# Next hgrn head's projections and gate chain between the present head's levels, with a second buffer set

## The chip, the core and the metric

The kernel runs on one core of one Trainium2 chip, as one launch. The metric is the device time of that execution in microseconds. The core has five engines that run in parallel, each in its own order: TensorE (PE, matmuls; its weight loads are PEld), VectorE (DVE), ScalarE (ACT), GpSimd (POOL) and SyncE (SP, here the issuer of weight loads). They meet at semaphores: an instruction that waits holds up all that is queued behind it on its engine. PSUM is the memory that matmuls write; everything else works in SBUF.

## The reference, cut to what matters

Two blocks run one after the other on a sequence of 512 tokens of width 1024. The first has two layers of mixed attention. The second, where the change lies, has three branches from one normalised input `h`, gated and summed, and then an FFN:

```python
o_a = dsa_attention(...)                    # sparse attention over selected keys
o_b = hgrn2_mixer(bq, bf, bi, bg, ...)      # 4 heads, gated linear recurrence in chunks of 64
o_c = mla_attention(...)                    # latent attention, 4 heads
gates = jax.nn.sigmoid(gate_logits)         # 3 x 1024 columns of h @ w_in
mixed = g_a * (o_a @ w_up_a) + g_b * (o_b @ w_up_b) + g_c * (o_c @ w_up_c)
x = x + mixed @ w_out                       # then the FFN and a last norm
```

Of the hgrn branch, for each head (keys and values of 128):

```python
log_f = jnp.logaddexp(log_lb, jnp.log1p(-lb) + jax.nn.log_sigmoid(fr))
k_in = (1.0 - lb) * jax.nn.sigmoid(-fr)
b = jnp.cumsum(lfc, axis=2)                                  # within a chunk
o_inter = jnp.einsum('bhck,bhkv->bhcv', qc * jnp.exp(b), state)
attn = jnp.einsum('bhtk,bhsk,bhtsk->bhts', qc, kc, decay)    # decay = exp(b_t - b_s), s <= t
new_state = exp(b_last) * state + einsum(kc * exp(b_last - b), vc)
o = rms_norm(o, out_gain) * jax.nn.silu(g)
```

## The kernel before

All activations stand transposed, with the feature on the 128 partitions and the 512 tokens along the row. `plan` writes out one list of steps by hand, and each engine's program is a walk through that list (`for op, arg in steps`) that takes from each step the part that is its own. So the order of steps is the order of every engine's queue.

**Groups.** A PE product that fills one PSUM bank is a `group`. There are two banks, `proj0` and `proj1`, used in turn: group g waits until whoever reads group g-2 has read it. A projection of 8 slabs of input (K=8) is 24 matmuls of 128x512 (L1436), since operands are split into a rounded part and a rest: high by high, high by low, low by high. Its weights come by one DMA of SP (L1316, 512 KB), are rounded by ACT (L1900) and subtracted by POOL (L1378) into the rest; `place_splits` puts that rounding (`split`) into the list some two groups ahead, but never ahead of the step in a slab's `after`.

**One hgrn head** has these steps, all of them 128x512:
- Projections of its queries (`hgrn_q`, "hq") and forget logits (`hgrn_f`, "hf"), evacuated by ACT (L1683).
- The gate chain: `hg_gate_a` part 0 on ACT (L1640 to L1642: abs, exp, ln), `hg_gate_d` part 0 on DVE (L2281 to L2283), `hg_gate_a` part 1 on ACT (L1866, then L1640 to L1642), `hg_gate_d` part 1 on DVE (L2288 to L2291, with a scan over tokens).
- Levels -1 to 5. The decay within a chunk is split by powers of two: for a level, DVE takes differences (`hg_diff`, L2300, L2301), ACT exponentials (L1872, L1873), DVE multiplies queries and keys by them (`hg_level`, L2314, L2315), PE multiplies these 4 times 128x128 (`hg_attn`, L1503), and DVE copies the product under a mask into the head's scores (`hg_put`, L2325). `hgrn_level` asks for the factors of the level after the one whose product it issues.
- The end: `hg_decay` (ACT L1880, L1881; DVE L2332, L2333), `hg_turn` (PE L1509, ACT L1731), two `hg_state` groups (PE L1519), `hg_chain` (DVE L2342, L2344), the head's gate projection `hgrn_gate` with silu (ACT L1640 to L1642, DVE L1997, ACT L1748, DVE L2047), `hg_out` (PE L1528, L1532; ACT L1733, L1737), `hg_meansq` (PE L1472), `hg_norm` (ACT L1646, L1647; DVE L2354), `gate3` (DVE L2057).

In `hgrn_state` and `hgrn_out` the next head's two projections and its gate chain stand between these.

**Tail gates.** The 24 K=8 projections of the branch gates ("sigmoid" groups) are spread evenly over the jobs. Gate i is copied by ACT into one of two buffers (L1729), goes through abs, exp, ln (ACT), min and subtract (DVE L2039) and exp (ACT L1745) in the steps `sig_ln`, `sig_min`, `sig_out` of the next gates, and is stored by a DMA of POOL (L1374). Its buffer serves gate i+2, whose copy waits for that DMA.

**Attention.** 16 tiles of latent attention (kind M) and 16 of sparse attention (kind X) run as a pipeline: `tick` issues one step of it, scores of tile n (PE L1572 to L1574 or L1576), softmax on DVE and ACT (L2095 to L2127, L1770; L2108, L2109, L1767), transposes of tile n-3 (PE L1588, ACT L1792), product with the values of tile n-4 (PE L1602). `weave` hands out ticks between jobs by a credit that each job's weight earns. All 32 tiles are through during the second head, at 1324 us.

**After it.** The step `tail` on ACT waits for all of this. Then ACT and DVE split ya, and the `up` groups follow.

## Time and profile before

| | us |
|---|---|
| median of the runs (2034.4 to 2037.26) | 2035.2 |
| profiled execution, its own time | 2032.24 |
| its span | 2030.4 |
| PE busy, of the span | 1764.3 (87%) |
| DVE busy | 847.8 (42%) |
| ACT busy | 805.0 (40%) |
| POOL busy | 590.5 (29%) |

Busy time counts an engine's instructions of work; waiting for a semaphore is not in it. The clock column (PEclk) is the mean of TensorE's granted clock in a stretch, 1 being full. An idle time in brackets stands behind the row that it ended with, with the engine and line that released it. Of a wait for several semaphores the last one is named. In the chain of work that ended last, 69% of the span is PE, 13% DVE, 8% ACT. Tile names are those of memory, so the same name can be different things: `weights` is the arena in which hgrn's buffers lie, `constants` also the tail gates, `h_tok` also the latent attention's queries and keys, `E` and `index_and_shared` two more buffers.

### The profile page before, as it was taken

The page shows a single profiled execution, that of the slowest core. Times are in us where ns is not written, and L with a number is a line of the kernel's source. Part 1 is how long each engine was busy: PE and PEld are TensorE (multiplying, and loading weights), DVE is VectorE, ACT ScalarE, POOL GpSimd, SP SyncE. Part 2 cuts the span into 40 slices and gives each one's busy share as a digit, 9 for nine tenths or more (in the row PEclk, how much of TensorE's full clock was granted, in tenths as well). Part 3 has the DMA queues.
Part 4 walks back from the last instruction along what each step waited for, and adds up shares of the span by engine and source line. Part 5 has one row for each costly group of instructions (what it writes and reads, how often), then busy time and mean ns, then how long its engine had stood idle before and what let it go on. Part 6 is the DMA issues. An engine that isn't in the chain of part 4 may idle for free.

```text
span 2030.4 us, 20883 instructions
## 1 busy us (share of the span) xinstructions
PE 1764.3 (87%) x7694; PEld 1325.3 (65%) x7694; DVE 847.8 (42%) x1477; ACT 805.0 (40%) x1512; POOL 590.5 (29%) x291
## 2 busy tenths in 40 slices
PE   4899998889989988889979968867769879999997
PEld 3666765667757656676636657656557658888886
DVE  4363345453433453544983536242326312212401
ACT  2234447322344563433324545453443324434411
POOL 4332211144122211422201222131236424444540
PEclk8898999999989988899989989888879989999999
DMA  5312221023132201231212222221245323333221
GB/s 172 88 42 63 63 59 57 22 64 93 32 82 54 83 32 43 88 82 33 60 36 58 73 73 63 60 66 48 66 132 185 103 62 100 98 94 101 86 94 42
DMA packets 204115, 149.83 MB, mean 74 GB/s; under 512 B 14956, under 2 KB 183536, under 8 KB 204016
## 3 DMA queue, kind: packets, MB, share of 16 engines
q1 hardware_dynamic: 199488, 133.57, 23.3%
q0 software_dynamic: 4528, 14.95, 2.4%
q8 instruction: 62, 1.02, 0.2%
q14 instruction: 37, 0.30, 0.0%
HBM read 138.00 MB, written 10.49 MB: 73 GB/s over the span
## 4 chain that ended last, share of the span: by engine, by line
PE 69%; DVE 13%; ACT 8%; issue 4%; DMA 3%; SPq 1%; POOL 0%; ACTq 0%; DVEq 0%
PE proj L1436 39%; PE proj L1432 12%; PE attn_out L1602 3%; PE score L1559 3%; PE score L1622 2%; PE turned_probs L1588 2%; PE proj L1622 1%; ACT weights_rounded L1900 1%; PE attn_out L1622 1%; DMA weights_raw<-in_w_in 1%; DVE small L2157 1%; DMA gates<-constants 1%; SPq L1316 1%; DVE rel_bias L2070 1%; PE score L1563 1%
## 5 line engine op out<-in xcount | busy, mean ns | idle before, releaser
L1378 POOL TENSOR_TENSOR weights_rounded<-weights_raw,weights_rounded 128x1024 fp32r<-128x1024 f32 (+1 forms) x237 | 562.8, 2392 | 1140.3 <-ACT weights_rounded L1900 1140.2
L1436 PE MATMUL proj<-hT_high,weights_rounded 128*128 128x512 f32 x2336 | 785.7, 410 | 47.4 <-DVE weights L2325 16.6
L1436 PEld LDWEIGHTS proj<-hT_high,weights_rounded 128*128 128x128 f32 x2336 | 456.9, 196 | 163.3 <-issue 20.4
L1436 PE MATMUL proj<-hT_low,weights_rounded 128*128 128x512 f32 x1168 | 468.9, 401 | 0.0
L1900 ACT ACTIVATE weights_rounded<-weights_raw 128x1024 fp32r<-128x1024 f32 (+1 forms) x237 | 233.9, 1009 | 161.1 <-DMA weights_raw<-in_w_ffn_down 57.8
L1436 PEld LDWEIGHTS proj<-hT_low,weights_rounded 128*128 128x128 f32 x1168 | 229.2, 196 | 50.4 <-issue 4.7
L1432 PE MATMUL proj<-weights_rounded,hT_high 128*128 128x512 f32 (+1 forms) x640 | 212.3, 409 | 43.8 <-DVE hT_low L1981 21.0
L1432 PEld LDWEIGHTS proj<-weights_rounded,hT_high 128*128 128x128 f32 x640 | 127.9, 203 | 77.3 <-issue 23.4
L1588 PE MATMUL turned_probs<-constants,probs 128*128 128x128 f32 x320 | 62.1, 296 | 43.4 <-ACT probs_T L1792 43.0
L1640 ACT ACTIVATE tg<-proj 128x512 f32<-128x512 f32 x42 | 25.1, 598 | 177.0 <-PE proj L1436 177.0
L1559 PE MATMUL score<-qk 64*128 64x256 f32 (+3 forms) x256 | 81.0, 495 | 11.0 <-DVE qk L1975 8.2
L1602 PE MATMUL attn_out<-probs_T,V 128*64 128x128 f32 (+1 forms) x560 | 89.5, 295 | 0.0
L1602 PEld LDWEIGHTS attn_out<-probs_T,V 128*64 128x64 f32 (+1 forms) x560 | 70.1, 173 | 10.9 <-issue 9.2
L1432 PE MATMUL proj<-weights_rounded,hT_low 128*128 128x512 f32 (+1 forms) x192 | 75.5, 393 | 0.0
L2019 DVE SCALAR_TENSOR_TENSOR tg<-proj,tg 128x512 f32<-128x512 f32 x22 | 15.2, 692 | 142.2 <-ACT tg L1642 142.2
L1436 PE MATMUL proj<-branches_high,weights_rounded 128*128 128x512 f32 x192 | 61.8, 398 | 13.0 <-POOL weights_rounded L1378 10.8
L1588 PEld LDWEIGHTS turned_probs<-constants,probs 128*128 128x128 f32 x320 | 37.6, 150 | 51.7 <-DVE probs L2127 30.6
L1374 POOL DMA_DIRECT2D gates<-constants x24 | 13.3, 556 | 198.8 <-ACT constants L1745 198.6
L2089 DVE TENSOR_REDUCE small<-score 128x1 f32<-128x128 f32 (+3 forms) x64 | 28.3, 484 | 92.8 <-PE score L1563 92.8
L1997 DVE SCALAR_TENSOR_TENSOR tg<-proj,tg 128x512 f32<-128x512 f32 x20 | 13.8, 692 | 125.2 <-ACT tg L1642 125.2
L1683 ACT ACTIVATE qk<-proj 128x512 f32<-128x512 f32 x32 | 19.1, 597 | 109.7 <-PE proj L1436 109.7
L1559 PEld LDWEIGHTS score<-qk 64*128 64x128 f32 x256 | 30.0, 192 | 45.7 <-issue 32.0
(371 smaller groups left out, 2463.6 us busy)
## 6 DMA issues: line engine op xcount, KB each, us to landing
weights_raw<-in_w_in SPq DMA_DIRECT2D x113, 512.0 KB, 4.1
weights_raw<-in_w_out SPq DMA_DIRECT2D x24, 512.0 KB, 3.8
weights_raw<-in_w_ffn_gate SPq DMA_DIRECT2D x22, 512.0 KB, 3.8
weights_raw<-in_w_ffn_up SPq DMA_DIRECT2D x22, 512.0 KB, 3.8
weights_raw<-in_w_ffn_down SPq DMA_DIRECT2D x22, 512.0 KB, 3.6
gates<-constants POOLq DMA_DIRECT2D x24, 256.0 KB, 2.4
weights_raw<-gates SPq DMA_DIRECT2D x24, 256.0 KB, 3.9
weights_raw<-in_w_in SPq DMA_DIRECT2D x20, 256.0 KB, 3.1
```

The costliest lines, as they stand in the source:

```text
L1316: sp.dma_start(dst, src).then_inc(p["loaded"], 16)
L1378: nc.gpsimd.tensor_tensor(piece_view(WR, p, "raw"), piece_view(WF, p, "raw"), piece_view(WR, p, "high"), ALU.subtract).then_inc(w_low, 1)
L1432: mm = nc.tensor.matmul(ps[:, 0:gr["N"]], x_[:, k, t * P:(t + 1) * P], w_[:, 0:gr["N"]], start=first, stop=last)
L1436: mm = nc.tensor.matmul(ps[:, :], w_[:, c0:c0 + P], x_[:, k, :], start=first, stop=last)
L1559: nc.tensor.matmul(ps[:, 0:K], qk[r, it["q"], tq], qk[r, it["k"], 0:K], start=True, stop=False)
L1563: mm = nc.tensor.matmul(sc[b % SCORE_BANKS][:, K - P:K], identb[:, :], negb[:, int(kind == "C"), :], start=False, stop=True)
L1588: mm = nc.tensor.transpose(T[:, j * P:(j + 1) * P], PR[:, i % 3, j * P:(j + 1) * P], cn("ident"))
L1602: mm = nc.tensor.matmul(O[u % 2][r0:r0 + rn, t * P:(t + 1) * P], v, PT[:, i % 2, j * P:(j + 1) * P], start=(j == 0), stop=(j == t))
L1622: mm = nc.tensor.matmul(down[2 * t + half][:, :], x_[c][:, t * P:(t + 1) * P], w_[:, 512 * half:512 * half + 512], start=(c == 0 and j == ...
L1640: link(nc.scalar.activation(dst, src, ACT.Abs, **kw))
L1900: nc.scalar.activation(piece_view(WR, p, "high"), piece_view(WF, p, "raw"), ACT.Copy).then_inc(w_high, 1)
L2089: ins = nc.vector.tensor_reduce(nmax[:, c + j:c + j + 1], sc[(first_map[n] + j) % SCORE_BANKS][:, 0:K], AX, ALU.max, negate=True)
```

## The change

Where the code puts the next head's two projections and its gate chain is new: between the levels of the present head, instead of in its end. For this a second set of the buffers b, k and q of a head is taken (`by_head`, in `E` and in `X2`, read in the traces as `index_and_shared`), and the chain no longer uses hG and hKE. The credit of `weave` gives way to `paced`, in which each job has a number of ticks written beside it, and the tail gates stand at written places: two between the levels of a head, and up to four in its end (after level 5, after the states, after the output, after the squares). All attention tiles are now spread over the four heads. The masked copy of a level comes ahead of the next level's factors. The last two tail gates are projected after the step `tail`, behind the split of ya, and the last steps of both stand between the first `up` groups. One more buffer is cleared once, and level 0 of a head waits for the output of the head before.

```diff
+    def paced(jobs, new_items):
+
+        add_items(new_items)
+        for fn, ticks in jobs:
+            fn()
+            for _ in range(ticks):
+                if state["n"] < len(items) + DRAIN:
+                    tick()
...
     def hgrn_level(h, lv):
 
+        put_back()
         if lv + 1 < LEVELS:
             steps.append(("hg_level", (h, lv + 1)))
             steps.append(("hg_diff", (h, lv + 2)))
         else:
             steps.append(("hg_decay", h))
-        g = group("hg_attn", head=h, level=lv)
+        hold["put"] = group("hg_attn", head=h, level=lv)
+
+    def hgrn_turn(h):
         put_back()
-        hold["put"] = g
+        group("hg_turn", head=h)
+        if h < 3:
+            steps.append(("hg_diff", (h + 1, 0)))
 
     def hgrn_state(h):
-        group("hg_turn", head=h)
-        put_back()
-        if h < 3:
-            hgrn_q(h + 1)
-        gs = [group("hg_state", head=h, part=i) for i in range(2)]
-        if h < 3:
-            hgrn_f(h + 1)
-        steps.append(("hg_chain", (h, gs)))
-        hold["states"] = gs
-        if h < 3:
-            steps.append(("hg_gate_a", (h + 1, 0)))
-        hold["g"] = hgrn_gate(h)
-        if h < 3:
-            steps.append(("hg_gate_d", (h + 1, 0)))
+        hold["states"] = [group("hg_state", head=h, part=i) for i in range(2)]
+        steps.append(("hg_chain", (h, hold["states"])))
 
     def hgrn_out(h):
-        hold["hgout"] = group("hg_out", head=h, states=hold["states"])
-        if h < 3:
-            steps.append(("hg_gate_a", (h + 1, 1)))
+        group("hg_out", head=h, states=hold["states"])
+
+    def hgrn_meansq(h):
         group("hg_meansq", head=h)
+
+    def hgrn_norm(h):
         steps.append(("hg_norm", h))
         steps.append(("gate3", hold["g"]))
-        if h < 3:
-            steps.append(("hg_gate_d", (h + 1, 1)))
-            steps.append(("hg_diff", (h + 1, 0)))
...
+        put_back()
+        hold["g"] = group("gate", slab("hgrn", c0=HG + 128 * h), K=KD, chunk=4 + h, layer=l, first=False, unit=None)
+
+    def gate_step(h, *what):
+        if h < 4:
+            steps.extend((name, (h, part)) for name, part in what)
+
+    def next_f(h):
+        if h < 4:
+            put_back()
+            hgrn_f(h)
+
+    def next_q(h):
+        if h < 4:
+            put_back()
+            hgrn_q(h)
+            gate_step(h, ("hg_gate_a", 0))
+
+    given = [0]
 
     def tail_gate(i):
-        gate_ready(i - 2)
-        gate_logs(i - 1)
-        gate_out(i - 2)
+        for what, n in (("sig_min", i - 2), ("sig_ln", i - 1), ("sig_out", i - 2)):
+            if 0 <= n < N_GATES:
+                steps.append((what, n))
         if i < N_GATES:
             put_back()
             group("sigmoid", slab("gate2", at=1024 * TAIL_ORDER[i // 8] + 128 * (i % 8)), K=KD, nth=i)
...
+    def next_gate():
+        tail_gate(given[0])
+        given[0] += 1
...
-    weave(jobs, its)
-    for i in (N_GATES, N_GATES + 1):
-        tail_gate(i)
+    jobs = []
+    for h in range(4):
+        last = h == 3
+
+        def level(lv, ticks, h=h):
+            jobs.append((lambda: hgrn_level(h, lv), ticks))
+            if h == 1 and 0 <= lv < NT:
+                jobs.append((lambda: steps.append(("masked", lv)), 0))
+
+        level(-1, 1)
+        jobs.append((lambda h=h: next_f(h + 1), 0))
+        level(0, 1)
+        jobs.append((lambda h=h: next_q(h + 1), 0))
+        level(1, 0)
+        jobs.append((next_gate, 0))
+        jobs.append((lambda h=h: gate_step(h + 1, ("hg_gate_d", 0)), 0))
+        level(2, 1)
+        jobs.append((lambda h=h: gate_step(h + 1, ("hg_gate_a", 1)), 0))
+        level(3, 0)
+        jobs.append((next_gate, 1))
+        jobs.append((lambda h=h: gate_step(h + 1, ("hg_gate_d", 1)), 0))
+        level(4, 0)
+        jobs.append((lambda h=h: hgrn_gate(h), 1))
+        level(5, 1)
+        jobs.append((lambda: steps.append(("gate2", hold["g"])), 0))
+        jobs.append((next_gate, 0))
+        jobs.append((lambda h=h: hgrn_turn(h), 1))
+        jobs.append((lambda h=h: hgrn_state(h), 1))
+        jobs.append((next_gate, int(last)))
+        jobs.append((lambda h=h: hgrn_out(h), int(last)))
+        if not last:
+            jobs.append((next_gate, 0))
+        jobs.append((lambda h=h: hgrn_meansq(h), int(last)))
+        if not last:
+            jobs.append((next_gate, 0))
+        jobs.append((lambda h=h: hgrn_norm(h), 0))
+    paced(jobs, its)
     flush()
-
-
-    new_rings(RINGS_TAIL)
     state["after"] = ("tail", 0)
     steps.append(("tail", 0))
+    steps.append(("split_x", ("ya", 0, 4)))
+    while given[0] < N_GATES:
+        next_gate()
+    new_rings(RINGS_TAIL)
...
+            if b == 0 and c in (0, 2):
+                next_gate()
...
-        hF, hA, hK, hQ = (qk[:, 4 + i, :] for i in range(4))
-        hB, hG, hQD, hKE, hATT = (X[:, i, :] for i in range(5))
+        hF, hA = qk[:, 4, :], qk[:, 5, :]
+        hB0, hG, hQD, hKE, hATT = (X[:, i, :] for i in range(5))
+        by_head = [(hB0, qk[:, 6, :], qk[:, 7, :]), (E[:, 0, 1, :], E[:, 1, 1, :], ikT)]
...
@@ -1862,9 +1891,10 @@
                         wait_group(hf_group[h])
                         log1p_exp_abs(hA, hF).then_inc(hg_act, 1)
                     else:
+                        _, hK, _ = by_head[h % 2]
                         act.wait_ge(hg_dve, 2 * h + 1)
-                        nc.scalar.activation(hG, hB, ACT.Exp)
-                        log1p_exp_abs(hKE, hA).then_inc(hg_act, 1)
+                        nc.scalar.activation(hK, hK, ACT.Exp)
+                        log1p_exp_abs(hF, hA).then_inc(hg_act, 1)
...
+                    if lv == 0 and h:
+                        dve.wait_ge(group_full, out_group[h - 1] + 1)
```

What this does to the queues shows in three places. First, DVE behind the end of head 0. Before, three steps of head 1's chain stand between the gate's product (L2047) and a softmax tile:

```order
L2342 COPY raw<-proj 128x128
L2344 SCALAR_TENSOR_TENSOR raw<-raw,small,proj 128x128 x6
L1997 SCALAR_TENSOR_TENSOR tg<-proj,tg 128x512
L2047 TENSOR_TENSOR tg<-proj,tg 128x512
L2281 SCALAR_TENSOR_TENSOR qk<-qk 128x512
L2282 TENSOR_TENSOR weights<-qk 128x512
L2283 TENSOR_SCALAR qk<-qk,small 128x512
```

The state chain, the gate and then head 1's `hg_gate_d` part 0 stand in a row. A little later, still DVE before, from the norm on:

```order
L2354 SCALAR_TENSOR_TENSOR y<-y,small,tg 128x512
L2057 TENSOR_TENSOR y<-y,tg 128x512
L2288 TENSOR_SCALAR qk<-qk,small 128x512
L2289 TENSOR_TENSOR weights<-weights,qk 128x512
L2290 SCALAR_TENSOR_TENSOR weights<-chunk_keep,weights 128x512
L2291 TENSOR_SCALAR qk<-weights,small 128x512
L2300 TENSOR_TENSOR weights<-weights 128x256
L2301 TENSOR_TENSOR weights<-weights 128x256
```

Part 1 of the chain stands between the head's output and the first difference of head 1. Now, DVE from the state chain of head 0 to the first levels of head 1:

```order
L2380 COPY raw<-proj 128x128
L2382 SCALAR_TENSOR_TENSOR raw<-raw,small,proj 128x128 x6
L2126 TENSOR_REDUCE small<-score 128x1
L2127 TENSOR_SCALAR small<-small 128x1
L2151 RECIPROCAL small<-small 128x1
L2158 TENSOR_SCALAR probs<-E,small 128x384
L2070 SCALAR_TENSOR_TENSOR constants<-constants,gate_logs 128x512 x3
L2392 SCALAR_TENSOR_TENSOR y<-y,small,tg 128x512
L2088 TENSOR_TENSOR y<-y,tg 128x512
L2351 TENSOR_TENSOR weights<-index_and_shared,weights 128x256
L2352 TENSOR_TENSOR weights<-E,weights 128x256
L2334 TENSOR_TENSOR weights<-E 128x256
```

The chain is gone from here; three tail gates (L2070) stand in its place, and the first level follows the output at once. The chain of head 1 is found further up on DVE, between levels of head 0:

```order
L2362 COPY_PREDICATED weights<-level_masks,proj 128x512
L2313 SCALAR_TENSOR_TENSOR E<-qk 128x512
L2314 TENSOR_TENSOR E<-E,qk 128x512
L2315 TENSOR_SCALAR qk<-E,small 128x512
L2351 TENSOR_TENSOR z<-qk,weights 128x32x8
L2352 TENSOR_TENSOR z<-qk,weights 128x32x8
L2334 TENSOR_TENSOR weights<-weights 128x256
L2335 TENSOR_TENSOR weights<-weights 128x256
```

`hg_gate_d` part 0 (L2313 to L2315) has moved between the masked copy of level 1 and the factors of level 3, and writes to `E`.

Second, ACT at the end of head 0. Now the outputs of head 0 stand among tail gates:

```order
L1758 ACTIVATE constants<-proj 128x512
L1762 ACTIVATE y<-proj 128x512
L1766 ACTIVATE tg<-y 128x512
L1669 ACTIVATE gate_logs<-constants 128x512
L1670 ACTIVATE gate_logs<-gate_logs 128x512
L1671 ACTIVATE gate_logs<-gate_logs 128x512
L1774 ACTIVATE constants<-constants 128x512
L1758 ACTIVATE constants<-proj 128x512
L1931 ACTIVATE weights_rounded<-weights_raw 128x1024
L1669 ACTIVATE gate_logs<-constants 128x512
L1670 ACTIVATE gate_logs<-gate_logs 128x512
L1671 ACTIVATE gate_logs<-gate_logs 128x512
```

Before, this was the same engine and place:

```order
L1767 ACTIVATE E,small<-logits,small 128x128
L1792 ACTIVATE probs_T<-turned_probs 128x256
L1733 ACTIVATE y<-proj 128x512
L1737 ACTIVATE tg<-y 128x512
L1866 ACTIVATE weights<-weights 128x512
L1640 ACTIVATE weights<-qk 128x512
L1641 ACTIVATE weights<-weights 128x512
L1642 ACTIVATE weights<-weights 128x512
L1900 ACTIVATE weights_rounded<-weights_raw 128x1024
L1646 ACTIVATE tg<-proj,small 128x512
L1647 ACTIVATE tg<-tg 128x512
L1872 ACTIVATE weights<-weights 128x256
```

The four steps of head 1's chain (L1866, L1640 to L1642) have gone, and copy, logarithms and exponential of the tail gates have come between output and norm.

Third, ACT ahead of the `up` groups. Before:

```order
L1729 ACTIVATE constants<-proj 128x512
L1640 ACTIVATE gate_logs<-constants 128x512
L1641 ACTIVATE gate_logs<-gate_logs 128x512
L1642 ACTIVATE gate_logs<-gate_logs 128x512
L1745 ACTIVATE constants<-constants 128x512 x2
L1916 ACTIVATE branches_high<-y 128x2048
L1900 ACTIVATE weights_rounded<-weights_raw 128x512 x9
```

and now:

```order
L1947 ACTIVATE branches_high<-y 128x2048
L1669 ACTIVATE gate_logs<-constants 128x512
L1670 ACTIVATE gate_logs<-gate_logs 128x512
L1671 ACTIVATE gate_logs<-gate_logs 128x512
L1774 ACTIVATE constants<-constants 128x512
L1931 ACTIVATE weights_rounded<-weights_raw 128x1024 x2
L1758 ACTIVATE constants<-proj 128x512
L1669 ACTIVATE gate_logs<-constants 128x512
L1670 ACTIVATE gate_logs<-gate_logs 128x512
L1671 ACTIVATE gate_logs<-gate_logs 128x512
L1774 ACTIVATE constants<-constants 128x512
L1758 ACTIVATE constants<-proj 128x512
```

The split of ya (L1916, now L1947) has moved ahead of the last two tail gates, and the rounding of those gates' weights stands behind it.

## Rows read from the trace of the kernel before

**Rows 1.** Windows: us, then busy (x) of PE, PEld, DVE, ACT, POOL; PEclk; DMA.

```profile
1081.30:1508.20 426.90, 327.81 (x1562) 260.33 (x1560) 174.36 (x364) 199.18 (x384) 95.94 (x63) 0.89 0.23 66
1081.30:1170.40 89.10, 81.73 (x396) 61.06 (x394) 44.48 (x103) 42.31 (x93) 20.67 (x13) 0.96 0.23 63
1170.40:1215.80 45.40, 28.25 (x143) 22.18 (x143) 18.29 (x41) 19.98 (x39) 9.27 (x7) 0.87 0.26 81
1215.80:1283.20 67.40, 60.58 (x321) 49.07 (x320) 35.40 (x84) 37.19 (x83) 14.62 (x10) 0.96 0.21 59
1283.20:1332.10 48.90, 29.86 (x151) 24.59 (x151) 13.96 (x26) 19.91 (x33) 9.98 (x5) 0.84 0.18 49
1332.10:1378.90 46.80, 39.12 (x181) 32.47 (x181) 21.38 (x38) 22.91 (x42) 14.52 (x9) 0.91 0.24 68
1378.90:1420.90 42.00, 31.15 (x136) 24.88 (x135) 11.61 (x20) 16.15 (x25) 7.67 (x4) 0.88 0.21 57
1420.90:1470.80 49.90, 35.61 (x157) 29.39 (x157) 19.77 (x39) 25.24 (x46) 14.60 (x10) 0.83 0.23 69
1470.80:1508.20 37.40, 21.52 (x87) 16.68 (x87) 9.48 (x15) 15.48 (x24) 4.60 (x5) 0.72 0.31 98
```

**Rows 2.** Waits of PE in 1081.3:1508.2: us in total, times, longest us.

```profile
PE turned_probs L1588 <- ACT probs_T L1792: 25.0, 9, 9.7
...
PE proj L1472 <- ACT tg L1737: 12.0, 4, 6.8
...
PE proj L1436 <- POOL weights_rounded L1378: 10.8, 1, 10.8
```

**Rows 3.** Costliest groups of PE there: busy us, mean ns, idle before.

```profile
L1436 PE MATMUL proj<-hT_high,weights_rounded 128*128 128x512 f32 x544 | 192.7, 428 | 30.3 <-DVE weights L2325 16.6 <-DVE raw L2344 11.0 <-ACT constants L1729 2.8
```

**Rows 4.** Chain that ended last, at head 2: start us, us, what.

```profile
1352.07 5.55 PE proj L1436 x24
```

**Rows 5.** Timeline, PE and ACT: start us, us, what, idle before.

```profile
1352.20 0.39 PE L1436 MATMUL proj<-hT_low,weights_rounded 128*128 128x512 f32 x1
...
1502.74 1.89 ACT L1916 ACTIVATE branches_high<-y 128x2048 fp32r<-128x2048 f32 x1
...
1508.18 0.76 PE L1436 MATMUL proj<-branches_high,weights_rounded 128*128 128x512 f32 x1 [10.82 <-POOL weights_rounded L1378]
```

**Rows 6.** Timeline of DVE at the end of head 0, and PE behind it.

```profile
1191.87 0.56 DVE L2095 TENSOR_REDUCE small<-score 128x1 f32<-128x384 f32 x1
...
1192.74 0.48 DVE L2127 TENSOR_SCALAR probs<-E,small 128x256 f32<-128x256 f32 x1
...
1205.56 1.70 DVE L2354 SCALAR_TENSOR_TENSOR y<-y,small,tg 128x512 f32<-128x512 f32 x1 [7.70 <-ACT tg L1647]
...
1207.98 0.54 DVE L2288 TENSOR_SCALAR qk<-qk,small 128x512 f32<-128x512 f32 x1
...
1213.83 0.45 PE L1588 MATMUL turned_probs<-constants,probs 128*128 128x128 f32 x1 [9.75 <-ACT probs_T L1792]
```

**Rows 7.** Timeline of ACT around one gate of the tail.

```profile
1153.38 0.61 ACT L1745 ACTIVATE constants<-constants 128x512 f32<-128x512 f32 x1
...
1157.24 0.60 ACT L1729 ACTIVATE constants<-proj 128x512 f32<-128x512 f32 x1 [3.25 <-DMA gates<-constants]
...
1160.82 1.04 ACT L1900 ACTIVATE weights_rounded<-weights_raw 128x1024 fp32r<-128x1024 f32 x1
```

**Rows 8.** Timeline of the decay's product on DVE twice, and of POOL.

```profile
1145.84 2.92 POOL L1378 TENSOR_TENSOR weights_rounded<-weights_raw,weights_rounded 128x1024 fp32r<-128x1024 f32 x1 [7.73 <-ACT weights_rounded L1900]
...
1146.44 2.88 DVE L2333 TENSOR_TENSOR qk<-qk,weights 128x512 f32<-128x512 f32 x1
...
1266.78 0.68 DVE L2333 TENSOR_TENSOR qk<-qk,weights 128x512 f32<-128x512 f32 x1
```

**Rows 9.** Costliest groups of DVE in 1081.3:1508.2.

```profile
L2300 DVE TENSOR_TENSOR weights<-weights 128x256 f32<-128x256 f32 x22 | 15.7, 712 | 0.8
...
L2354 DVE SCALAR_TENSOR_TENSOR y<-y,small,tg 128x512 f32<-128x512 f32 x4 | 5.9, 1475 | 42.4 <-ACT tg L1647 42.4
```

66 lines of the change are left out of this document (22 added, 44 removed).

## The prediction

> **What bounds the kernel now.** The page's first part has TensorE (PE) busy for 87% of the span and no other engine over 42%, so I look for the places where PE stands. The diff touches only the stretch from the first product of the hgrn levels (1081.3 us) to the first up projection (1508.2), so I cut that into windows: for each of the four heads its levels, and its end (turn, states, next head's projections, gate, output, norm) [rows 1]. In the whole stretch PE is busy 327.8 of 426.9 us, hence idle 99.1. No other engine comes near: ACT 199.2, DVE 174.4, POOL 95.9. So PE bounds it, through the waits between its groups. By difference the idle time is 7.4, 6.8, 7.7 and 14.3 us in the four levels (36.2 together), 17.1, 19.0 and 10.9 in the first three ends (47.0), and 15.9 in the last. The waits of PE say on what [rows 2]: 25.0 us before the transposes of the softmax, which are behind DVE and ACT at a head's end, 12.0 on the squares for the head's norm, 10.8 before the first up projection.
>
> The half clock takes more. Over the stretch it is 0.89 [rows 1], so of the two levels, 2.4 and 1.2 GHz, the lower was granted for 22%, 94 us. The 544 matmuls of the projections on hT_high last 428 ns on average [rows 3]; one at the upper level lasts 0.39 us and at the lower 0.76, and 24 in a row at the upper level take 5.55 us, 0.23 each from start to start [rows 4, 5]. The excess, 544 x 0.038 = 21 us of duration, and half as much again for the 272 on hT_low, makes 31 / 0.37 = 84 matmuls at half speed. Each steps 0.23 slower: 19 us, and with some of it on attention and levels about 25. In proportion that is 0.25 us for each idle us (an estimate: the clock fell in and behind the idle places), and leaves about 303 us of work at full clock. The change keeps this work: 34 projections of 24 matmuls (24 gates, 10 of hgrn), 28 level products, 32 attention tiles, four ends.
>
> **The change, part by part.**
>
> 1. *Projections of the next head, and its gate chain, leave the end.* Today the end holds two of PE's K=8 groups for the next head, and DVE has seven instructions for its chain, the last four (L2288 to L2291) just before the first level of the next head, from 1207.98, after a norm of 1.70 that waited 7.70 for ACT; PE stands meanwhile, idle 9.75 us before the transposes at 1213.83 [rows 6]. All of it moves under the levels at no cost of PE time, since each step there stands between two projections of 5.55 us; ACT's logarithms (three of 0.63 and an exponential) go along, in ACT's queue behind the evacuation of the projection. The second buffers (E, X2, the fourth slot of qk) are what lets it. Added: one memset before the stretch, which I cost at nothing because DVE is idle there between topk rounds; uncovered it is below 1 us, for head 0 only. No DMA is added. SP's loads keep their distance of two groups, so their landings stay hidden by the projections ahead.
>
> 2. *Level steps.* They keep their order, with the masked copy now always ahead of the next level's factors. PE's products need factors made one job earlier, so a projection covers the chain. What remains is ACT's queue: a gate evacuation (L1729) waits for the DMA of the gate two before it. From the exponential before (1153.38 + 0.61) it starts at 1157.24, 3.25 us later, POOL's issue included [rows 7]. A gate's turn on ACT is then 0.60 (copy) + 1.04 (rounding the next weights) + 3 x 0.63 + 0.61 + 3.25 = 7.4 us, against 5.55 of projection. Whenever other PE work between two gates is under 1.9 us, a bank is freed late. Walking the new order through one head with these durations gives 1.0 us before the product of level 3, 2.4 before the gate projection, and about 1 of crumbs: 4.5. Head 0, with few tiles yet, 4; head 3, with no next head to project, 0.8 + 2 + 1.6 and the rest of a chain that is bare in places, 9. Together 22 against 36.2. Bounds: nothing, to 14.3 for each head, the bare chain of head 3 today [rows 1].
>
> 3. *The end of heads 0 to 2.* (a) The gate group's bank is freed by DVE's product L2047, which now stands behind the decay and two attention tiles. From the end of that projection: three logarithm steps of 0.63 on ACT, 0.69 on DVE (a 128x512 pass of either is 0.60 to 0.69, [rows 6 to 8]), a softmax tile on DVE 1.3 (0.56 + 0.48 and two one-column steps, [rows 6]), its exponential and copy on ACT some 0.9, the decay's exponentials 0.85 and products 2 x 0.68, the next tile with its exponential 1.9, then 0.63 and 0.69: 10 us, against two tiles and a product on PE, some 5.4. Idle 4.6. (b) The chain of states (2.75 today, twice a bank wait on DVE) has a tile as cover: 0. (c) Three gates then stand between turn, output and squares. The first two have 3 to 4 us beside them; the third follows a short group, and its bank is 1.4 late. (d) Level -1 of the next head needs the bank of the squares, which ACT frees only behind the third gate's copy: 3.3. Sum 9.3 for each, 28 for three against 47.0. Bounds: 5 (only a) to 19.0 (as today).
>
> 4. *The last end.* Two gates move behind the tail step, and with them the rounding of their weights, since the planner puts a slab made after `tail` behind it. So after the last squares PE waits for ACT root 1.3, DVE norm and gate 1.5 to 2.4, ACT's copy of ya 1.89 [rows 5], logarithms 1.9, exponential 0.6, rounding 1.04, POOL 2.4: with waits between them 11.5, less 0.8 for the last transposes, 10.7 us idle. Today's 10.82 before the first up projection [rows 5] falls to some 3.3, because ya is split by then, and 1.3 more before the second. With (a) at 5.6 (sparse tiles are longer on DVE) and 1 before the squares: 22 against 15.9. This part loses 6. Bounds: 11 if the wait before the last two gates is hidden, 26 if that wait and today's 15.9 simply add.
>
> *Sum.* Idle 22 + 28 + 22 = 72, against 99.1: 27 less. At 0.25 for the clock that gives 7 more. **34 us.** The profiled execution took 2032.2 (span 2030.4), so 1998; it stands 3 under the median of the runs, 2035.2, from which 34 leaves **2001**.
>
> *A rule against it.* Where DVE reads two SBUF tensors while POOL subtracts, it is stretched: L2333 took 2.88 us beside a subtraction of 2.92, and 0.68 without [rows 8]. The Trainium skill, GPSIMD Engine Reference, section "Key points", has it that GpSimd shares its SBUF interfaces with VectorE and contends with such instructions; this trace agrees, at 2.88 against 0.68. The change puts the chain and levels nearer to the subtractions. By the rows what is stretched today lies in the idle times that I counted, and 34 stands; by the rule at its worst it is the third rival.
>
> **The rivals.**
>
> *Fuller cover.* If my late banks in levels are covered by PE work that I set too short, levels cost 8 instead of 22, and the ends 5 each: idle 8 + 15 + 22 = 45, 54 less, with the clock 67: 1968. For it: head 0's levels, with a tile in nearly every step, have only 7.4 idle at 0.96 clock [rows 1]. Against: the gate's turn of 7.4 us stands in ACT's queue wherever the tiles stand. 0.15.
>
> *Waits change places.* Attention is spread to the end, so heads 2 and 3 get DVE and ACT work in levels that now run bare. If each level stretch then costs what head 3's costs now, 14.3, idle is 57 + 28 + 22 = 107, 8 more: 2045. With half of that growth it is 89. For it: the two heads without attention have as much idle per level time as those with it [rows 1]. Against: the factors of a level are made one job ahead of its product in the new order. That half would be 2023. Counted under "no change": 0.08.
>
> *Slower, by stretched DVE.* POOL's 35 subtractions in the stretch each last 2.4 us. If each catches one two-input DVE instruction on the chain at 2.88 - 0.68 = 2.2 us, that is 77 us, against 10 now in the two kinds most stretched: 22 x (0.71 - 0.42) + 4 x (1.48 - 0.69) [rows 9]. It decides from 34 / 1.25 = 27 us exposed, twelve more such hits where PE waits. At full price, 67 x 1.25 = 84 less 34: 2085; at half, 2043. 0.09. For it: the norm L2354 was stretched to 1.70 in the end that I cited, and there the two engines meet by plan. Against: with a projection of cover in each step a hit of 2.2 is mostly hidden.
>
> *It doesn't do what it says:* should the new waits on the previous head's output (level 0) or the gate DMA serialise head after head, the ends stay at 47: idle 91, 10 us won: 2025. 0.06.
>
> **How the numbers follow.** Forecast 0.62 (1980 to 2020), fuller cover 0.15, little won 0.06, waits change places 0.08, slower 0.09. The range for 8 in 10 takes half of the fuller cover and of the little won: 1974 to 2031. A measurement here tells 0.2% (4 us) from no change. Faster by more: 0.62 + 0.15 + 0.06 and 0.02 of the waits that change places, 0.85; within 0.2%: 0.05 of those; slower: 0.09 and the last 0.01 of them, 0.10.
>
> **What would show it.** In the profile after: the stretch from first level product to first up projection 427 - 34 = 393 us long, PE idle about 72 in it, clock 0.91 to 0.93; the 9.75 before the transposes gone; 3 to 6 us before the gate that follows level 5; 2 to 4 before each head's level -1; some 11 us between the last attention output and the last two gate projections, at a lowered clock; the first up projection under 5 us after them. Wrong if DVE's two-input instructions with over 2 us are more than half again as many, if ACT's evacuations of gates wait for DMA over 4 us each, or if the level stretches show over 10 us idle each.

## The result, and the profile after

| | before | after |
|---|---|---|
| median of the runs, us | 2036.2 (2034.4 to 2037.5) | 2002.6 (1997.4 to 2008.3) |
| ratio to before, 95% interval | | 0.9836 (0.9808 to 0.9864) |
| span of the profiled execution | 2030.4 | 2000.8 |
| first level product to first up projection | 426.9 | 393.4 |

The prediction said 2001, with 393 us for that stage. It had 2035.2 as the median before, from three of the four runs in this table; the four give 2036.2, so the change brought 33.6 us by the medians and 29.6 by the two profiled spans. The windows of the kernel after, which answer to [rows 1], first the whole stage, then levels and end of each head in turn, and last the 20 us behind the first up projection (columns: us, busy time with instructions of PE, PEld, DVE, ACT and POOL, PEclk, DMA share, GB/s; the first tail gate behind level 5 counts to the end):

```profile
1078.80:1472.20 393.40, 325.60 (x1562) 257.93 (x1560) 193.96 (x362) 191.62 (x375) 94.09 (x60) 0.90 0.23 66
1078.80:1128.00 49.20, 45.36 (x214) 35.15 (x213) 27.10 (x51) 22.08 (x47) 10.51 (x5) 0.93 0.24 64
1128.00:1170.90 42.90, 36.31 (x174) 27.58 (x172) 13.68 (x29) 23.27 (x43) 11.90 (x8) 0.92 0.23 65
1170.90:1226.20 55.30, 49.70 (x242) 38.88 (x243) 44.02 (x77) 26.62 (x56) 13.18 (x7) 0.94 0.24 65
1226.20:1271.60 45.40, 36.67 (x175) 27.86 (x173) 13.73 (x30) 23.28 (x43) 14.03 (x12) 0.92 0.34 108
1271.60:1325.00 53.40, 46.05 (x224) 38.57 (x225) 36.33 (x61) 26.71 (x56) 13.52 (x7) 0.90 0.25 67
1325.00:1370.40 45.40, 36.16 (x168) 28.57 (x166) 15.22 (x29) 23.35 (x43) 11.92 (x8) 0.89 0.22 62
1370.40:1411.00 40.60, 35.25 (x177) 29.12 (x178) 26.45 (x54) 20.07 (x45) 8.31 (x5) 0.87 0.22 61
1411.00:1472.20 61.20, 40.09 (x198) 32.19 (x196) 17.43 (x32) 26.24 (x46) 10.72 (x8) 0.83 0.13 44
1472.20:1492.20 20.00, 13.64 (x50) 10.43 (x51) 5.76 (x7) 9.09 (x14) 10.56 (x9) 0.89 0.80 249
```

PE's idle time in the stage is 393.4 - 325.6 = 67.8 us, where it was 99.1; 72 was predicted. Its work is the same 1562 matmuls. So of the 33.5 us that the stage is shorter, 31.3 are idle time and 2.2 are matmuls that ran faster (a second profile of the same kernel, below, has 29.1 and 5.0). Behind the stage, 6.4 us were lost again: from the first up projection to the end it is 528.6 us, and it was 522.2. In the last window above PE is idle 6.4 us; in the 20 us behind the first up projection before, it was busy 19.53. The start of the stage lies 2.5 earlier, but that is chance: in the kernels of this study, which hardly differ up to there, it lies between 1072.7 and 1083.5. The waits of PE in the stage, to be read beside [rows 2] (us in total, times, longest):

```profile
PE proj L1465 <- DVE tg L2078: 15.8, 4, 4.1
PE proj L1465 <- POOL weights_rounded L1407: 12.7, 1, 12.7
PE proj L1465 <- ACT constants L1758: 10.4, 7, 2.7
PE turned_probs L1617 <- ACT probs_T L1821: 6.7, 6, 2.2
PE proj L1532 <- ACT tg L1676: 6.3, 3, 2.1
PE proj L1532 <- ACT constants L1758: 5.0, 2, 2.9
...
PE proj L1501 <- ACT tg L1766: 0.2, 1, 0.2
```

Line numbers are some 30 higher now: L1465 is the projection, L1532 the level product, L1617 the transposes, L1501 the squares of the norm, L1758 ACT's copy of a tail gate, L2078 DVE's product for the head's gate. The 25.0 us before transposes are 6.7 now, and the 12.0 before the squares 0.2. What is left is mostly the banks. Where it stands in time (start us, us, what, idle before):

```profile
1132.61 0.79 PE L1465 MATMUL proj<-hT_high,weights_rounded 128*128 128x512 f32 x1 [3.85 <-DVE tg L2078]
...
1170.92 1.16 PE L1532 MATMUL proj<-index_and_shared,E 128*128 128x128 f32 x8 [2.10 <-ACT tg L1676]
...
1455.96 0.77 PE L1465 MATMUL proj<-hT_high,weights_rounded 128*128 128x512 f32 x1 [12.69 <-POOL weights_rounded L1407]
1472.18 0.47 PE L1465 MATMUL proj<-branches_high,weights_rounded 128*128 128x512 f32 x1 [2.96 <-issue]
1481.32 0.77 PE L1465 MATMUL proj<-branches_high,weights_rounded 128*128 128x512 f32 x1 [3.36 <-issue]
1491.47 0.79 PE L1465 MATMUL proj<-branches_high,weights_rounded 128*128 128x512 f32 x1 [3.00 <-DVE V L2035]
```

These are the places that the prediction named: (a) before the gate behind level 5, (d) before level -1, the two late gates, the first up projection. For the last two rows, 6.4 us together, it had one wait of 1.3.

### The profile page after: what moved, and what is told of

Read it like the earlier page. It is cut to its first block, busy times and chain, and to the rows that moved or that the text cites. A ratio compares the mean times of both kernels' runs of the same rounds, so it can differ in the third digit from the quotient of the medians.

```text
span 2000.8 us, 20884 instructions
## 1 busy us (share of the span) xinstructions
PE 1761.0 (88%) x7694; PEld 1321.8 (66%) x7694; DVE 875.5 (44%) x1478; ACT 803.1 (40%) x1512; POOL 586.4 (29%) x291
## 4 chain that ended last, share of the span: by engine, by line
PE 69%; DVE 13%; ACT 8%; issue 4%; DMA 4%; POOL 1%; SPq 1%; ACTq 0%; DVEq 0%
PE proj L1465 39%; PE proj L1461 13%; PE attn_out L1631 3%; PE score L1588 3%; PE score L1651 2%; DMA gates<-constants 2%; PE proj L1651 2%; PE turned_probs L1617 1%; ACT weights_rounded L1931 1%; DMA weights_raw<-in_w_in 1%; PE attn_out L1651 1%; DVE small L2188 1%; POOL weights_rounded L1407 1%; DVE rel_bias L2101 1%; PE proj L1471 1%
## 5 line engine op out<-in xcount | busy, mean ns | idle before, releaser
L1465 PE MATMUL proj<-hT_high,weights_rounded 128*128 128x512 f32 x2336 | 785.4, 410 | 60.0 <-POOL weights_rounded L1407 20.3
L1465 PEld LDWEIGHTS proj<-hT_high,weights_rounded 128*128 128x128 f32 x2336 | 456.4, 195 | 177.3 <-issue 31.9
L1465 PE MATMUL proj<-hT_low,weights_rounded 128*128 128x512 f32 x1168 | 469.1, 402 | 0.0
L1465 PEld LDWEIGHTS proj<-hT_low,weights_rounded 128*128 128x128 f32 x1168 | 229.1, 196 | 49.3 <-issue 3.9
L1617 PE MATMUL turned_probs<-constants,probs 128*128 128x128 f32 x320 | 59.8, 287 | 26.4 <-ACT probs_T L1821 26.2
L2050 DVE SCALAR_TENSOR_TENSOR tg<-proj,tg 128x512 f32<-128x512 f32 x22 | 15.2, 692 | 141.9 <-ACT tg L1671 141.9
L1465 PE MATMUL proj<-branches_high,weights_rounded 128*128 128x512 f32 x192 | 63.1, 406 | 11.5 <-issue 6.3
L1617 PEld LDWEIGHTS turned_probs<-constants,probs 128*128 128x128 f32 x320 | 36.6, 146 | 33.7 <-DVE probs L2158 14.1
L1793 ACT ACTIVATE E<-score,small 128x128 f32<-128x128 f32 (+3 forms) x64 | 33.2, 524 | 60.0 <-DVE small L2120 60.0
L1821 ACT ACTIVATE probs_T<-turned_probs 128x128 f32<-128x128 f32 (+3 forms) x128 | 54.2, 423 | 4.1 <-PE turned_probs L1617 4.1
```

Of the source, the lines that this page charges most:

```text
L1465: mm = nc.tensor.matmul(ps[:, :], w_[:, c0:c0 + P], x_[:, k, :], start=first, stop=last)
L1617: mm = nc.tensor.transpose(T[:, j * P:(j + 1) * P], PR[:, i % 3, j * P:(j + 1) * P], cn("ident"))
L1793: ins = nc.scalar.activation(e[:, j, :], sc[(first_map[n] + j) % SCORE_BANKS][:, 0:K], ACT.Exp, bias=nmax[:, c + j:c + j + 1], accum_out=s ...
L1821: nc.scalar.activation(PT[:, i % 2, 0:it["K"]], T[:, 0:it["K"]], ACT.Copy).then_inc(turned_out, 1)
```

## The experiments

Each starts from the kernel after, but for the last. The stage is counted from the first level product to the first up projection.

| kernel | median us | ratio to before (95%) | stage us | PE idle | PE busy | PEclk |
|---|---|---|---|---|---|---|
| before (profiled as above) | 2031 to 2033 | 1 | 426.9 | 99.1 | 327.8 | 0.89 |
| after_again | 2001.6 | 0.9843 (0.9813 to 0.9872) | 392.8 | 70.0 | 322.8 | 0.91 |
| chain_back | 2045.7 | 1.0067 (1.0042 to 1.0093) | 433.2 | 98.6 | 334.6 | 0.87 |
| tiles_early | 2031.2 | 0.9992 (0.9972 to 1.0012) | 424.3 | 89.9 | 334.5 | 0.88 |
| tail_undo | 1991.2 | 0.9799 (0.9777 to 0.9820) | 384.6 | 63.4 | 321.2 | 0.91 |
| tail_split | 1995.8 | 0.9827 (0.9799 to 0.9855) | 382.8 | 64.8 | 318.0 | 0.92 |
| gate2_early | 1999.1 | 0.9842 (0.9813 to 0.9871) | 390.2 | 66.1 | 324.1 | 0.91 |
| three_buffers | 1987.7 | 0.9783 (0.9752 to 0.9815) | 374.6 | 57.6 | 317.0 | 0.91 |
| three_tail | 1968.0 | 0.9694 (0.9663 to 0.9725) | 360.4 | 46.3 | 314.1 | 0.93 |
| gate2_three_tail | 1953.0 | 0.9612 (0.9590 to 0.9634) | 340.0 | 31.6 | 308.4 | 0.96 |
| all_late | 1954.7 | 0.9619 (0.9599 to 0.9639) | 338.4 | 32.5 | 305.9 | 0.97 |
| pool_light | 1992.0 | 0.9800 (0.9772 to 0.9828) | 380.0 | 60.2 | 319.8 | 0.92 |
| before_light | 2022.4 | 0.9949 (0.9929 to 0.9968) | 424.6 | 90.1 | 334.5 | 0.87 |

The common measure, the kernel after once more:

> The changed kernel as it is, timed beside the others, as their common measure: 0.984 of the kernel before, about 2002 us. Its stage from the first level product to the first up projection about 393 us, PE idle 68 in it.

It came to 2001.6, and its stage to 392.8 us. Two profiled executions of the same kernel thus differ by 2.2 us in idle time and 2.8 in busy time. Smaller differences in the table say nothing. The largest difference is in the levels of head 3, 5.4 us idle in the kernel after and 9.7 in after_again (the window as in the table of windows above, and a PE instruction in it):

```profile
1364.80:1407.10 42.30, 32.62 (x177) 26.95 (x178) 26.59 (x54) 20.07 (x45) 8.35 (x5) 0.96 0.21 59
...
1386.11 1.16 PE L1532 MATMUL proj<-z 128*128 128x128 f32 x8 [2.70 <-ACT constants L1758]
```

It is 42.3 us long instead of 40.6, at a granted clock of 0.96 instead of 0.87, with 32.6 us busy instead of 35.3. The 2.70 are for a gate's copy whose buffer was stored in 4.5 us; the same store took 2.3 in the kernel after. Where another engine sets the pace, slower matmuls fill time in which PE would else be idle, so idle and busy time of a short stretch can't be read apart.

### The two halves of the change

chain_back puts the next head's projections and chain back into the end:

```diff
     def hgrn_state(h):
+        if h < 3:
+            hgrn_q(h + 1)
         hold["states"] = [group("hg_state", head=h, part=i) for i in range(2)]
+        if h < 3:
+            hgrn_f(h + 1)
         steps.append(("hg_chain", (h, hold["states"])))
+        gate_step(h + 1, ("hg_gate_a", 0))
...
-        jobs.append((lambda h=h: next_f(h + 1), 0))
...
-        jobs.append((lambda h=h: next_q(h + 1), 0))
...
+        jobs.append((lambda h=h: gate_step(h + 1, ("hg_gate_d", 1), ("hg_diff", 0)), 0))
```

> Undoes the main part alone: the next head's two projections and its gate chain stand in the end of the present head again, at the places they had before (queries' projection before the states, forget logits behind them, chain around gate, output and norm). Second buffers, spread tiles, tail gates at their written places and the tail stay as in the changed kernel. Theory (the gain came from projections and chain under the levels): levels are barer and the next head waits for the chain again, 20 to 35 us slower than the changed kernel, that is as slow as the kernel before or slower. Rival (spread tiles and written places of the gates brought most of it): under 8 us slower.

It took 2045.7 us, 44 more than the kernel after and 0.67% more than before, above the 20 to 35 of the theory. The chain is bare between norm and level -1 again. Timeline of DVE and of PE in chain_back at the end of head 0:

```profile
1183.32 0.75 DVE L2393 SCALAR_TENSOR_TENSOR y<-y,small,tg 128x512 f32<-128x512 f32 x1 [15.18 <-ACT tg L1677]
...
1184.78 0.54 DVE L2322 TENSOR_SCALAR E<-E,small 128x512 f32<-128x512 f32 x1
1185.36 0.69 DVE L2323 TENSOR_TENSOR qk<-qk,E 128x512 f32<-128x512 f32 x1
1186.08 1.23 DVE L2324 TENSOR_TENSOR_SCAN E<-chunk_keep,qk 128x512 f32<-128x512 bf16 x1
1187.34 0.49 DVE L2325 TENSOR_SCALAR E<-E,small 128x512 f32<-128x512 f32 x1
...
1187.98 1.40 PE L1533 MATMUL proj<-index_and_shared,E 128*128 128x128 f32 x5 [6.57 <-DVE E L2325]
```

PE stands 6.57 us before the level, three times, and the first three ends have 56.5 us of idle time (18.9, 17.1 and 20.5, each counted from the last level product to the next head's first), where the kernel after has 28.2 by the same cuts. The levels cost it hardly more: 18.7 against 16.3.

tiles_early has double ticks, so that the tiles are through early in head 2:

```diff
-            for _ in range(ticks):
+            for _ in range(2 * ticks):
...
-            if h == 1 and 0 <= lv < NT:
-                jobs.append((lambda: steps.append(("masked", lv)), 0))
+            if h == 0 and 2 <= lv < 2 + NT:
+                jobs.append((lambda: steps.append(("masked", lv - 2)), 0))
```

> Undoes the spreading of the attention tiles alone: every job has twice the ticks, so that all 32 tiles are through early in head 2 as before, and heads 2 and 3 have none; everything else as in the changed kernel. Theory (projections of cover in the levels carry the gain): levels of heads 2 and 3 go from 5 and 5 us idle towards the 14 of the bare head before, their gate bank waits of 4 us go, 5 to 12 us slower than the changed kernel. Rival (the spreading is what brought the gain): 20 us slower or more. Third (tiles put DVE and ACT work in the way): faster.

The edit also has DVE wait, ahead of level 0, for the decay of the head before; DVE stands nowhere for that (no idle time before L2336 at level 0). It took 2031.2 us: 30 more than after, and within 0.2% of before. The theory had 5 to 12, so here the rival is right. Waits of PE in its stage:

```profile
PE turned_probs L1617 <- ACT probs_T L1821: 24.0, 12, 6.2
```

With two tiles in a row PE waits for softmax before transposes, as before the change (25.0, [rows 2]). The waits go where tiles stand close together: by the same cuts the levels of heads 1 and 2 have 12.8 and 9.9 us idle, where the kernel after has 4.9 and 5.1. So chain and tiles are not two gains that add. The new layout with the chain in the end is 13 us slower than before, the new layout with tiles early is as fast as before, and with both in their new places it is 33 faster (the late gates' part is in all three; by the next section it costs some 9 us, and no run has the chain or the tiles moved without it).

### The late gates

tail_undo projects all 24 tail gates before the step `tail`:

```diff
-        if not last:
-            jobs.append((next_gate, 0))
+        jobs.append((next_gate, 0))
         jobs.append((lambda h=h: hgrn_meansq(h), int(last)))
-        if not last:
-            jobs.append((next_gate, 0))
+        jobs.append((next_gate, 0))
...
     paced(jobs, its)
+    for i in range(2):
+        next_gate()
     flush()
...
-            if b == 0 and c in (0, 2):
-                next_gate()
```

> Undoes the tail part alone: in the changed kernel the last two tail gates are projected in the end of head 3, like those of other heads, and closed ahead of tail; the split of ya still stands right behind tail. By the prediction's step 4 (this part loses 6 us of idle time, 21 to 23 against 16): 5 to 9 us faster than the changed kernel. Rival (without projections behind tail the whole chain of norm, split and rounding is bare before the first up projection, as the 10.8 us were before, and the gates add their own waits): as slow or slower.

It was 9 us faster than after by the ratios (0.9799 against 0.9843) and 10 by the medians, at the upper end of the theory's 5 to 9; the two intervals just touch. The gap stands before the first up projection now:

```profile
1461.29 0.77 PE L1462 MATMUL proj<-branches_high,weights_rounded 128*128 128x512 f32 x1 [12.73 <-POOL weights_rounded L1404]
```

It is one gap of 12.73 instead of 12.69 + 2.96, and PE is then busy for all of the 20 us behind it. So the tail part of the change costs, as step 4 said, and the 6.4 us of idle time among the first up groups are part of it. How the rest divides can't be read here: the profiled execution took 1980.9 us, 10 less than the median of its runs.

tail_split asks what the gap of 12.7 is. This is ACT in the kernel after, from the last norm to the gates (start, us, what, idle before):

```profile
1445.00 1.91 ACT L1947 ACTIVATE branches_high<-y 128x2048 fp32r<-128x2048 f32 x1 [1.09 <-DVE y L2088]
1449.93 0.63 ACT L1669 ACTIVATE gate_logs<-constants 128x512 f32<-128x512 f32 x1 [3.02 <-DVE constants L2070]
1450.59 0.63 ACT L1670 ACTIVATE gate_logs<-gate_logs 128x512 f32<-128x512 f32 x1
1451.25 0.63 ACT L1671 ACTIVATE gate_logs<-gate_logs 128x512 f32<-128x512 f32 x1
1451.79 0.61 ACT L1774 ACTIVATE constants<-constants 128x512 f32<-128x512 f32 x1
1452.31 1.99 ACT L1931 ACTIVATE weights_rounded<-weights_raw 128x1024 fp32r<-128x1024 f32 x2
```

It is the chain that the prediction added up (1.89 + 1.9 + 0.6 + 1.04), with one term more: the 3.02, in which the logarithms wait for DVE. DVE first makes the low part of ya and only then the minimum:

```profile
1446.94 2.29 DVE L2401 TENSOR_TENSOR branches_low<-y,branches_high 128x2048 fp32r<-128x2048 f32 x1 [2.06 <-ACT branches_high L1947]
1449.15 0.69 DVE L2070 SCALAR_TENSOR_TENSOR constants<-constants,gate_logs 128x512 f32<-128x512 f32 x1
```

The prediction left L2401 out. The edit moves one line, so that the two gates' slabs no longer carry `tail`:

```diff
     flush()
-    state["after"] = ("tail", 0)
     steps.append(("tail", 0))
     steps.append(("split_x", ("ya", 0, 4)))
     while given[0] < N_GATES:
         next_gate()
+    state["after"] = ("tail", 0)
```

> Only this: the weights of the last two tail gates are rounded where the list would put them without the step tail, among the last tiles of head 3, instead of behind tail and the split of ya. Theory (the 12.7 us of idle PE before these two gates are the wait for ACT's rounding, which stands in ACT's queue behind tail, the split of ya, three logarithm steps and an exponential): the gap falls below 1 us, the two projections then cover norm, split of ya and its low part, and the kernel is 12 to 15 us faster than the changed kernel (about 1988). Rival (the gap belongs to the last norm and to the copies of the banks, the rounding only ends last in it): another wait of 7 us or more takes its place, 0 to 5 us faster.

The gap before the gates was gone, but only 3 to 6 us were won, and the interval overlaps that of after_again. PE and ACT in tail_split:

```profile
1458.19 0.60 ACT L1758 ACTIVATE constants<-proj 128x512 f32<-128x512 f32 x1 [6.77 <-DMA gates<-constants]
...
1460.75 0.77 PE L1465 MATMUL proj<-branches_high,weights_rounded 128*128 128x512 f32 x1 [13.53 <-issue]
```

The rival was right: another wait took its place. ACT's copy of the last gate waits for the store of gate 21 to free the buffer. The exponential that the store waits for began at 1450.81 and took 0.61; the copy started at 1458.19. The loads of the up weights run beside the store, as the window between shows (DMA share 0.94; PE idle, at half clock):

```profile
1450.00:1458.00 8.00, 0.00 (x0) 0.00 (x0) 0.00 (x0) 1.39 (x3) 0.54 (x1) 0.50 0.94 306
```

The copy before this one had to wait only 2.88 for its store. The rounding of the up weights stands in ACT's queue behind this copy.

### Buffers, and the head gate's bank

In the kernel after, ACT waits longest for such stores (us, times, longest): 

```profile
ACT constants L1758 <- DMA gates<-constants: 53.5, 16, 5.6
```

three_buffers gives the gates a third buffer, in the latent queries of head 0:

```diff
-            return cn(("sin1", "cos1")[i % 2])
+            return cn(("sin1", "cos1")[i % 3]) if i % 3 < 2 else flat[:, 0, :]
...
-                        if i >= 2:
-                            act.wait_ge(gates_out[i % 2], 16 * (i // 2))
+                        if i == 2:
+                            act.wait_ge(scores_full, first_X_head)
+                        if i >= 3:
+                            act.wait_ge(gates_out[i % 3], 16 * (i // 3))
```

> In the changed kernel, tail gates use three buffers in turn instead of two (the third lies over the latent queries of head 0, which are no longer read; the quarter of x that returns to that place is loaded during the up projections). ACT's copy of gate i then waits for the store of gate i-3, not i-2. Theory (ACT's 53 us of waiting for stores lie in the queue ahead of level steps, of the norm's root and of bank copies, and PE waits for those): the third gates' bank waits (0.5, 2.6, 2.1), those before level -1 (2.1 three times) and several of levels go, 8 to 15 us less idle, 8 to 18 us faster. Rival (ACT has slack there, its other work of 4.1 us a gate is below 5.55 of projection and the wait is only where it rests): 0 to 4 us faster. The gap of 12.7 before the last two gates stays in both.

By the medians 14 us faster than after_again, by the ratios 12, with 12 us less idle time: the theory. ACT's wait for stores is gone from its profile altogether. Those waits had grown from 31.8 us before (12 of them) to 53.5 not only because the gates stand closer: of the stores issued in the stage, one took over 3 us to land before (beside two at its very end, 6.7 and 7.0), and seven did in the kernel after, up to 5.2 us. The gap before the late gates stayed, and so did (a), 15.8 us in four waits, and (d), 1.93 each instead of 2.10.

three_tail is three_buffers with the edit of tail_split:

> Three buffers as in the run before, and the last two gates' rounding not held behind tail. With two buffers that moved the gap of 12.7 to one of 13.5 before the first up projection, where ACT's copy of the last gate waited 6.8 us for the store of gate 21, which lay among the loads of the up weights. Theory (that store is all that replaced the gap): with the third buffer the gap before the first up projection is under 4 us, 12 to 18 us faster than with three buffers alone. Rival (the up weights' loads, 18 of 256 KB at once, or their rounding end just as late): gap of 8 us or more, under 6 us faster than three buffers alone.

A further 20 us, more than the theory's 12 to 18. The gap before the first up projection is 3.65:

```profile
1436.79 0.47 PE L1470 MATMUL proj<-branches_high,weights_rounded 128*128 128x512 f32 x1 [3.65 <-issue]
```

So the two edits, 14 and 5 apart, bring 34 together: the gap that tail_split had moved to a wait for a store is closed by the third buffer.

gate2_early takes up (a):

```diff
+        jobs.append((lambda: steps.append(("gate2", hold["g"])), 0))
         level(5, 1)
-        jobs.append((lambda: steps.append(("gate2", hold["g"])), 0))
```

> In the changed kernel, only the head gate's exponential and product (the step gate2) come one job earlier: right behind the gate projection and its tile, ahead of the decay and the last level's product. Theory (the idle 3.9 to 4.1 us of PE before the first tail gate of each end is the wait for a bank that DVE frees only behind the decay and a tile): the four gaps go, 16 us less idle, 12 to 20 us faster than the changed kernel (about 1985). Rival (ACT's logarithms, or the decay that then comes later, end next): the wait moves to the transposes of the turned keys or to the state products, under 5 us faster.

2.5 us by the medians and nothing by the ratios: the rival. Waits of PE in its stage:

```profile
PE proj L1548 <- ACT qk L1760: 15.2, 4, 4.5
...
PE proj L1465 <- DVE tg L2078: 0.7, 4, 0.2
```

The wait for L2078 went from 15.8 to 0.7, as meant, and one of 15.2 us came before the state products, for ACT's copy of the turned keys. That copy stands behind a tail gate's copy, which waited for its store. With the third buffer it should not. gate2_three_tail joins the three edits:

> Three buffers, the last two gates' rounding not held behind tail, and the head gate's product one job earlier. Alone, the last of these moved the wait of 3.9 us from the first tail gate of an end to the state products, where PE waited 3.5 to 4.5 us for ACT's copy of the turned keys; that copy stood behind a tail gate's copy, which waited for a store. Theory (with a third buffer nothing holds ACT there): both waits are gone, 14 to 16 us less idle PE than with three buffers and early rounding alone, 12 to 20 us faster (about 1951). Rival (the logarithms of the gate or the decay come late in any order): under 5 us faster.

```profile
1076.00:1416.00 340.00, 308.38 (x1562) 246.47 (x1560) 194.61 (x362) 191.58 (x375) 94.36 (x60) 0.96 0.26 76
```

1953.0 us, 15 less than three_tail and 2 from the theory's number. With all_late below, which does not differ from it, this is the fastest kernel of the study, 0.9612 of before, and nothing is left out in it. (a) is worth nothing in the kernel after and 15 us here.

all_late moves the closing steps of the last two gates:

```diff
-            if b == 0 and c in (0, 2):
+            if b == 0 and c in (4, 6):
```

> As the run before, and the closing steps of the last two tail gates (logarithms, exponential, store) stand behind the fifth and seventh up group instead of the first and third. Theory (the idle 3.4 and 2.9 us among the first up groups, 0.5 in the kernel before, are ACT's logarithms of these gates ahead of the rounding of up weights, and DVE's ya and yb parts behind them): the 3.4 goes, 3 to 6 us faster than the run before. Rival (these gaps come of the late loads and of the split of yb): 0 to 1 us.

No difference (1954.7); the rival. A wait of 3.7 before the first up projection and one of 4.1 for DVE (L2042) behind it stand in its profile, where gate2_three_tail has 3.7, 3.4 and 2.8. The theory of the ups' gaps, ACT's logarithms, explains one of them at most. What else holds them is open; tail_undo, which has no gates behind `tail`, has none of them.

### DVE beside POOL

pool_light writes zeros where POOL subtracts, for hgrn's and the gates' weights, so the low part of these weights is left out:

```diff
+                    if slabs[p["slab"]]["name"] in ("gate2", "hgrn"):
+                        nc.gpsimd.memset(piece_view(WR, p, "raw").bitcast(F32), 0.0).then_inc(w_low, 1)
+                    else:
```

> In the changed kernel POOL writes zeros instead of subtracting, for the weights of hgrn and of the tail gates (the low part of these weights is left out, the matmuls on it stay). Measures what POOL's two-input subtractions cost DVE in this stage, the mechanism of the third rival. Theory (stretched DVE instructions are mostly covered): DVE's busy time in the stage falls from 194 us to 165 to 175, the kernel is 2 to 5 us faster than the changed kernel, 1 to 2 of it from the gap of 12.7, which ends with a subtraction. Rival (stretched DVE is on the path): 10 us faster or more.

The stage of pool_light:

```profile
1081.60:1461.60 380.00, 319.83 (x1561) 254.02 (x1559) 157.56 (x362) 191.17 (x375) 46.63 (x59) 0.92 0.24 68
```

DVE's busy time fell from 194.0 to 157.6 us, and 9 to 10 us were won (0.9800 against 0.9843; the intervals overlap a little), 1.4 of them in the gap of 12.7, which was 11.3. So at least 36 us of DVE's time in the stage are stretching, and up to 8 us of the kernel hang on it: nearer to the rival's size than to the theory's. Up to, because POOL's own work became shorter too (94.1 to 46.6 us), which frees the low parts of the weights and POOL's queue earlier; no run separates the two. What is stretched most is not what the third rival looked at. Groups of DVE, in after and in pool_light (busy us, mean ns, idle before):

```profile
L2158 DVE TENSOR_SCALAR probs<-E,small 128x128 f32<-128x128 f32 x8 | 12.5, 1560 | 0.3
L2352 DVE TENSOR_TENSOR z<-E,weights 128x256 f32<-128x256 f32 x6 | 6.9, 1144 | 0.0
```

```profile
L2161 DVE TENSOR_SCALAR probs<-E,small 128x128 f32<-128x128 f32 x8 | 3.2, 394 | 0.3
L2355 DVE TENSOR_TENSOR z<-E,weights 128x256 f32<-128x256 f32 x6 | 2.5, 421 | 0.0
```

The same edit to the kernel before:

> The kernel before with POOL writing zeros instead of subtracting for the weights of hgrn and of the tail gates (their low part is left out, the matmuls on it stay). In the changed kernel this took DVE's busy time in the stage from 194 to 158 us and 10 us off the whole. Theory (the change brought more of DVE's two-input instructions and softmax products under POOL's subtractions): DVE falls only from 174 to about 158, and the kernel is 2 to 6 us faster than before. Rival (as much on the path in both, the change added nothing on it): 9 us or more faster than before.

```profile
1079.80:1504.40 424.60, 334.52 (x1561) 264.80 (x1560) 158.33 (x364) 199.76 (x386) 48.69 (x62) 0.87 0.24 70
```

DVE fell from 174.4 to 158.3 us, as expected, but 9 to 10 us were won here too (0.9949), so the rival holds. The change raised the stretching from 16 to 36 us, and leaving the subtractions out is worth the same, about 10 us, in both.

## Why the prediction was right

| step | predicted | measured |
|---|---|---|
| levels of the four heads, PE idle | 4, 4.5, 4.5, 9 = 22 | 3.8, 5.6, 7.4, 5.4 = 22.1 |
| ends of heads 0 to 2 | 9.3 each = 28 | 6.6, 8.7, 9.2 = 24.6 |
| (a) gate behind level 5 | 4.6, last head 5.6 | 3.9, 3.9, 4.1, 4.1 |
| (b) chain of states | 0 | 0, 0, 1.0 |
| (c) third gate | 1.4 | 0.5, 2.6, 2.1 |
| (d) before level -1 | 3.3 | 2.1, 2.1, 2.1 |
| last end, to the first up projection | 22 with the next row | 21.1 |
| before the late gates | 10.7 | 12.7 |
| first up projection, then behind it | 3.3, 1.3 | 3.0, 3.4 + 3.0 |
| clock's gain in the stage | 7 | 2.2 (after_again 5.0) |
| stage, us | 393 | 393.4 |

*Mechanism.* That the time lay in PE's waits between groups, and that chain and projections under the levels would take those of the ends, is shown: chain_back gives it all back. But the prediction priced only this move. It never priced the spreading of the tiles, beyond a rival in which that does harm, and tiles_early shows that without the spreading nothing is left of the gain. The prediction's own case, "Forecast", is what happened, with a condition that it had not seen.

*Levels.* The sum is right, its parts less so: head 2 has 7.4 instead of 4.5, where two of the waits (2.9 and 2.2) are for ACT's copy of a gate, which had itself waited 4.9 and 3.7 for a store, and a third (2.2) is for the copy before the transposes. Head 3 has 5.4 instead of 9, but 9.7 in after_again, so its miss is chance as far as is known; by the same cuts the four levels of after_again add up to 24.7.

*Ends.* (d) was set too long by a third: from the end of the third gate's projection to the level there are only the gate's copy (0.60) and the two steps of the norm's root (0.68 and 0.63), 2.1 us in all. (a) was within 1 us. What the prediction did not say is that (a) is not a price by itself: gate2_early removed it and won nothing, as the copy of the turned keys came next. The terms of such a sum are what ends last, not what could be taken away one by one.

*The last end.* The chain of ACT's steps was right in kind and 2.0 short, the wait for DVE's minimum behind the low part of ya. The 1.3 behind the first up projection was the worst term: 6.4. "This part loses 6" is borne out by tail_undo, at 9 to 10.

*The clock.* This term was the one sized worst in the stage. The prediction took 0.25 us back for each idle us, as a constant: 7 us, at a granted clock of 0.91 to 0.93. It was 2.2 at 0.90, and 5.0 at 0.91 in after_again. The 544 matmuls on hT_high took 428 ns before ([rows 3]) and take 430 after:

```profile
L1465 PE MATMUL proj<-hT_high,weights_rounded 128*128 128x512 f32 x544 | 193.9, 430 | 45.2 <-DVE tg L2078 15.8 <-POOL weights_rounded L1407 12.7 <-ACT constants L1758 10.4
```

31.3 us less idle time brought 2.2 us of faster matmuls, 0.07 for each, and 0.17 in after_again. From after to gate2_three_tail, 36.2 us less idle time (67.8 to 31.6) brought 17.2 (325.6 to 308.4), 0.48 for each; from after_again it is 0.38. Over the whole way from before to gate2_three_tail it is 19.4 for 67.5, or 0.29, not far from the prediction's number. The windows show where: before, the levels of heads 0 and 1 ran at 0.96 and their ends at 0.87 and 0.84 ([rows 1]); after, it is 0.93 and 0.94 in the levels and 0.92 in both ends. The ends gained and the levels lost, and idle places of 2 to 4 us stand in all of them now. How many idle us there are does not give the clock from one kernel to the next: before_light and tiles_early both have 9 less than before and 6.7 us more busy time, more than the 2.8 by which two profiles of one kernel differ. So the price of an idle us holds at best on average over large changes, and not for a step of this size.

*How the errors met.* Idle time in the stage was 3 us better than predicted (67.8 against 70.7, as the 72 holds the 1.3 behind the first up projection), the clock 5 worse, and 5 more were lost behind the first up projection. From the span of before, 2030.4, the 33.5 and -6.4 leave 2003.3, and 2.5 of chance ahead of the stage give the 2000.8 that the profile shows. So the size and the places of the idle time were understood, but that the total came out within 2 us of 2001 is luck: the profiled pair has 29.6 us of gain where the medians have 33.6, and the runs of one kernel spread by more than that (1997.4 to 2008.3).

*The rivals.* Fuller cover, 1968, is what the schedule could have given: three_tail reaches it (46.3 us idle against the rival's 45), once no copy waits for a store, though by other parts: its last end has 11.6 us idle instead of the 22 that the rival left standing. "Against" had named the obstacle, the gate's turn of 7.4 us in ACT's queue. Its 3.25 of waiting for a store was taken there as a fixed part of the turn. In the kernel after, these waits are 53.5 us in 16 instead of 31.8 in 12, and a third buffer removes them. Slower by stretched DVE: the mechanism is there, its size had been seen in only two kinds of instruction (10 us, where before_light shows 16), and the added 20 us of stretching did not show in the time. That answers to the sentence "a hit of 2.2 is mostly hidden". None of the three signs of being wrong appeared: DVE's two-input instructions of over 2 us went from 7 to 9, below half again as many; ACT's 16 waits for stores are 3.3 us each on average, under 4; and no level stretch has over 10 us idle. The first sign looked at too little, though: with the one-tensor instructions counted, those of over 2 us went from 7 to 13.

## What to carry to other kernels

When work is moved under other work, look at what each moved copy waits for at its new place: a buffer whose store was in time at a loose spacing holds the whole queue at a tight one, and one more buffer was worth 12 to 14 us beside the 33 of the change. Two waits that stand one behind the other in a queue must be removed together before both show their full gain: 14 and 5 us apart were 34 together (by the medians), and the 15.8 us of (a) gave nothing until the third buffer was there. Spread the cover (here the attention tiles) over all of the bare places; moving the chain without that gave nothing, with the late gates' loss of 9 us in it.

## What the runs showed of the hardware that was not expected

Some kinds of DVE instruction that run into a subtraction of POOL end only with it, and instructions with one tensor are among them. In the kernel after, twelve of the softmax products (L2158, one tensor and a scalar column; 0.29 us for 128x128 where POOL is idle) run beside a subtraction of POOL that began before them or within 0.1 us; each of them ends 0.08 to 0.22 us after POOL's end, so they last 0.90 to 2.51 us. In the kernel before it is one. Not all kinds pay: beside the same subtractions sixteen steps of the state chain (L2382, which read PSUM) took 0.35 us each, and five reductions (L2140, from SBUF) 0.42 to 0.69, as they do elsewhere. A memset of POOL does it too: in pool_light one of these products took 0.94 beside a memset of 0.96. Timelines of DVE and POOL in after:

```profile
1130.31 1.64 DVE L2158 TENSOR_SCALAR probs<-E,small 128x128 f32<-128x128 f32 x1
...
1129.29 2.58 POOL L1407 TENSOR_TENSOR weights_rounded<-weights_raw,weights_rounded 128x1024 fp32r<-128x1024 f32 x1 [15.04 <-ACT weights_rounded L1931]
```

POOL ends at 1131.87 and DVE at 1131.95. The prediction had this only for instructions that read two tensors. The Trainium skill, GPSIMD Engine Reference, section "Key points", has it for DVE instructions that read two SBUF inputs and also for those in a mode that uses two ports; the products are of the second kind if their 0.487 us for 128x512, against 0.68 for a two-tensor pass, is that mode, and the trace then agrees with the page.

A store of 256 KB landed 2.3 us after its issue between loads of 512 KB that came one by one (the median of seven, 1300 to 1400 us), and held ACT for 6.77 us when the up weights were loaded at 306 GB/s. Executions of one kernel differ by up to 18 us in this case (2021.4 to 2039.1 among twenty of the kernel before, timed together); the start of the stage alone moved by 10 us among kernels that are nearly the same ahead of it.
